# Two moves in the mixing layers of a transformer kernel: the second half of a prepared norm, and the loads of the spatial gate

## The reference, cut to what matters

```
hx = modulated_norm(x, norm_g[l, 1], mx[3], mx[4])     # rmsnorm(x, g) * (1 + scale) + shift
hc = modulated_norm(ctx, norm_g[l, 1], mc[3], mc[4])
px = hx @ w_in[l]                                      # 1024 -> a, b, q, k, v, d and four gates
pc = hc @ w_in[l]                                      # the last layer takes only k and v of ctx
...
# sgu_branch: the spatial gate, b
u, v = split(gelu(p[..., B_OFF:Q_OFF]));  v = layernorm_plain(v)
s = einsum("gpq,bnqgc->bnpgc", w_s, vc) + b_s.T[:, :, None]
yb = (u * s) @ w_b_out
...
merged = g0 * ya + g1 * yb + g2 * yc + g3 * yd         # yc: differential attention over q, k, v
x = x + mx[5] * (merged @ w_o)
```

## Time and profile before

| | us |
|---|---|
| median of 3 runs | 4151.28 |
| the three runs | 4151.28, 4140.68, 4152.42 |
| the profiled execution | 4140.58 |
| its span | 4138.8 |
| TensorE busy | 3803.3 (92%) |
| weight loads busy | 3601.8 (87%) |
| GpSimd busy | 2664.1 (64%) |
| ScalarE busy | 1944.5 (47%) |
| VectorE busy | 1731.4 (42%) |

### The profile page before, as it was taken

The page is one execution under the profiler, slowest core; times in us unless marked ns, Lnnn a source line. Parts: engine busy times, 40 slices in busy tenths (PEclk is TensorE's granted clock), DMA queues, the critical chain, the costliest instruction groups (busy, mean ns, idle before and its releaser), DMA issues.

```text
span 4138.8 us, 93911 instructions
## 1 busy us (share of the span) xinstructions
PE 3803.3 (92%) x36101; PEld 3601.8 (87%) x36101; DVE 1731.4 (42%) x3388; ACT 1944.5 (47%) x2757; POOL 2664.1 (64%) x1186
## 2 busy tenths in 40 slices
PE   8998998997898889899999978879999999997899
PEld 7678987997698757899999868869999999996898
DVE  5543216316633643442222573673223222348442
ACT  5225447433444411545554454464555555545543
POOL 5007873875287300788887747638888888883776
PEclk9999999998899989999999989989999999998999
DMA  5555662663166345566666435426666666652564
GB/s 180 190 195 149 191 179 64 193 166 102 49 192 187 108 165 174 157 187 201 191 191 181 144 88 169 136 75 181 190 192 182 193 184 195 186 168 76 154 176 143
DMA packets 1162942, 664.79 MB, mean 161 GB/s; under 512 B 30157, under 2 KB 1122201, under 8 KB 1162551
## 3 DMA queue, kind: packets, MB, share of 16 engines
q1 hardware_dynamic: 1162679, 661.06, 54.3%
HBM read 659.92 MB, written 1.05 MB: 160 GB/s over the span
## 4 chain that ended last, share of the span: by engine, by line
PE 54%; issue 30%; POOL 11%; DVE 2%; ACT 2%; DMA 1%; POOLq 0%; SPq 0%; DVEq 0%; ACTq 0%
PE bank L855 52%; POOL wlo L615 11%; PE bank L834 1%; PE bank L1056 0%; ACT whi L625 0%; DMA raw<-in_w_in 0%; DVE OUTH L931 0%; PE bank L955 0%; ACT L1932 0%; DMA raw<-in_ffn_w_gu 0%; DVE sq L771 0%; DVE OUTL L933 0%; ACT bank L749 0%; ACT L1940 0%; ACT W L1932 0%
## 5 line engine op out<-in xcount | busy, mean ns | idle before, releaser
L615 POOL TENSOR_TENSOR wlo<-raw,whi 128x1024 fp32r<-128x1024 f32 (+3 forms) x1182 | 2663.9, 2270 | 1450.8 <-ACT whi L625 1444.1
L625 ACT ACTIVATE whi<-raw 128x1024 fp32r<-128x1024 f32 (+3 forms) x1182 | 1172.1, 995 | 1192.0 <-PE bank L855 1002.2
L855 PE MATMUL bank<-AH,whi 128*128 128x256 f32 (+1 forms) x5712 | 1608.5, 282 | 30.3 <-DVE AL L765 10.1
L855 PE MATMUL bank<-AL,whi 128*128 128x256 f32 x5712 | 1600.8, 280 | 0.0
L855 PE MATMUL bank<-AH,wlo 128*128 128x256 f32 (+1 forms) x5712 | 1599.2, 280 | 0.0
L855 PEld LDWEIGHTS bank<-AH,whi 128*128 128x128 f32 x5712 | 1094.8, 192 | 39.4 <-issue 16.5
L855 PEld LDWEIGHTS bank<-AL,whi 128*128 128x128 f32 x5712 | 1090.6, 191 | 0.7
L855 PEld LDWEIGHTS bank<-AH,wlo 128*128 128x128 f32 x5712 | 1089.9, 191 | 0.0
L855 PE MATMUL bank<-HH,whi 128*128 128x256 f32 x1936 | 537.9, 278 | 0.0
L855 PE MATMUL bank<-HL,whi 128*128 128x256 f32 x1936 | 535.9, 277 | 0.0
L855 PE MATMUL bank<-HH,wlo 128*128 128x256 f32 x1936 | 535.9, 277 | 0.0
(11 more groups left out here) (427 smaller groups left out, 5073.5 us busy)
## 6 DMA issues: line engine op xcount, KB each, us to landing
raw<-in_ffn_w SPq DMA_DIRECT2D x420, 512.0 KB, 3.9
raw<-in_w_in SPq DMA_DIRECT2D x182, 512.0 KB, 3.8
raw<-in_ffn_w_gu SPq DMA_DIRECT2D x176, 512.0 KB, 3.8
ada_raw<-in_w_ada SPq DMA_DIRECT2D x96, 512.0 KB, 5.9
raw<-in_ffn_w_down SPq DMA_DIRECT2D x64, 512.0 KB, 3.9
raw<-in_rw_w_rkv SPq DMA_DIRECT2D x48, 512.0 KB, 3.8
raw<-in_w_ada SPq DMA_DIRECT2D x48, 512.0 KB, 5.7
raw<-in_ffn_w SPq DMA_DIRECT2D x56, 384.0 KB, 3.4
```

The lines of the kernel that those rows point to most:

```text
L615: pool.tensor_tensor(wlo[slot][:, 0:n], raw[slot][:, 0:n], whi[slot][:, 0:n], ALU.subtract).then_inc(lo_ready, 1)
L625: act.activation(whi[slot][:, 0:n], raw[slot][:, 0:n], ACT.Copy).then_inc(hi_ready, 1)
L855: mm = pe.matmul(ps[:, 0:o.shape[2]], w, o[:, k0 + c, :], start=tile not in started and c == n == 0, stop=last_panel and c == nk - 1 and n ...
```

## The change

It has two parts. First, for the two hosts mix0c and mix0x the second piece of the prepared norm (the sums over partitions, the root, the reciprocal) stands behind the second tile of `.q` and no longer behind the fourth tile of `.k`. The squares stay behind the first tile of `.k`. TensorE and VectorE get the calls to do so in `.q`. mix1c, which has no `.q`, keeps its place. Second, in all three full mixing layers the spatial gate's loads are issued ahead of the panels of `.ab` and no longer ahead of those of `.q`.

```diff
         for host, name in (("mix0c", "mix0x"), ("mix0x", "f20c")):
-            SUMS_AT[f"{host}.k", 0] = ROOT_AT[f"{host}.k", 3] = name
+            SUMS_AT[f"{host}.k", 0] = ROOT_AT[f"{host}.q", 1] = name
...
-            pe_panels(pe, f"{pre}.q", fills=0)
+            pe_tiles_with_norm(pe, f"{pre}.q", pe_panels(pe, f"{pre}.q", fills=0, by_hand=True))
             pe_panels(pe, f"{pre}.v", fills=0)
...
             if full:
-                dve_tiles(dve, f"{pre}.q", take_copy(dve, DQ))
+                tile = dve_tiles(dve, f"{pre}.q", take_copy(dve, DQ), by_hand=True)
+                for st in range(G[f"{pre}.q"].steps):
+                    tile(st)
+                    dve_prepare(dve, f"{pre}.q", st)
+                dve.wait_ge(bank_free, tiles_of(f"{pre}.q"))
...
-                if g.name.endswith(".q") and g.name[:5] in [f"mix{l}{s}" for l, s in FULL]:
+                if g.name.endswith(".ab") and g.name[:5] in [f"mix{l}{s}" for l, s in FULL]:
                     sp_gated_unit(sp, int(g.name[3]))
```

## The result

The changed kernel takes 4127.98 us in the median of 10 runs (4109.39 to 4151.77), the kernel before 4151.85 in the median of 10. Nine of these ten lie between 4134.17 and 4160.82 us; the tenth took 5591.26, and why isn't known. The ratio of the runs without it is 0.9947, 95% interval 0.9922 to 0.9972: 22 us less, with 12 to 32 us inside the interval.

A forecast was written before the change was run, and what follows sets the result against it. TensorE, busy 3803.3 of 4138.8 us, was taken as the bound; 8.62 + 7.87 + 3.76 - 0.45 - 0.45 gave 19.3 us off, 4121.3 from the profiled execution, 4132 from the median; forecast 4130, range 4116 to 4142.

The forecast's parts named there:

- The cause and the two places in mix0c and mix0x: In mix0c and mix0x, gate loads ahead of the query's first panel make the squares late; removal saves 8.62 and 7.87 us.
- mix1x: In this layer, TensorE's 1.88 us wait ahead of the query and the lower clock behind it go: 3.76 us less.
- Part one gains nothing and costs a little: Sums, root and reciprocal behind the second query tile save nothing and add 0.45 us of wait each in mix0c and mix0x.
- The gate loads ahead of `.ab` cost nothing: At `.ab`'s first panel in three layers, the later issue was priced at nothing, with 3.6 us of cover on ScalarE.
- Rival A: `.ab`'s first panel comes late and TensorE waits in all three layers; gives back 11.3 us, time 4141; chance 8%.
- B: GpSimd's low parts become the bound in the query; gives back 6.6 us, time 4137; chance 8%.
- C: At `.ab`'s first tile, gate transfers hold up the panels behind them; net 6.6 us slower, time 4156; chance 3%.
- D: The query's first panel is late for another reason and the squares stay late; time 4150; chance 3%.
- The sum: Over the three full mixing layers, 8.62 + 7.87 + 3.76 - 0.45 - 0.45 = 19.35, say 19.3 us gained.
- The two levels of the runs: Of three runs of the kernel before, two lay near 4152 us and one near 4141, taken as distinct groups.

The follow-up runs named there:

- loads only: Kernel before with only the gate's loads moved ahead of `.ab`, sums, root and reciprocal left in place: median 4117.75 us, ratio 0.9942.
- root only: Kernel before with only sums, root and reciprocal moved behind the second query tile, gate's loads left ahead of `.q`: median 4137.00 us, ratio 0.9991.
- squares first: Kernel before, but in mix0c and mix0x ScalarE makes the squares ahead of rounding the query's first panel: median 4133.57 us, ratio 0.9973.
- wait left: Kernel before with SyncE's wait for `sgu_free` left ahead of `.q`, only the five gate loads moved ahead of `.ab`: median 4126.84 us, ratio 0.9960.
- six more loads: Changed kernel with six spare loads (640 KB) added behind the gate's five, ahead of `.ab`: one run, 4130.11 us, beside 4136.92 for the kernel before.
- second execution of the changed kernel: The changed kernel profiled again with nothing altered, on the chip of other experiments: median of 12 runs 4120.84 us, ratio 0.9953 to the kernel before.

## Why the prediction was right, point by point

- **The cause and the two places in mix0c and mix0x.** Right, and shown by loads only (all of it), root only (none), and squares first (the link through ScalarE). By the stages, mix0c gave 7.99 us where 8.62 - 0.45 = 8.17 were forecast, mix0x 7.26 where 7.42 were.
- **mix1x.** Forecast 3.76, measured 2.92. In three later profiles with the loads moved the stage takes 30.37 or 30.38 us, which is 34.56 - 30.37 = 4.19 less; in wait left it takes the 31.64 of the first again. The wait is gone in all. What differs is the pace of the tiles, which I had taken as one number, 2.72 us. That 3.76 lies between the two is chance.
- **Part one gains nothing and costs a little.** Right. The wait at the second query tile is 0.26 us instead of 0.45, and the clock stayed at 1.00. The place costs more than its wait, as the tile behind it ran at the slower pace. Counted at 2.72 us a tile, the stages of loads only would be 32.9 to 33.0 us, an estimate from its trace; with both parts they are 33.5. So the term is near 0.5 us a place. It is too small to be told by the timing.
- **The gate loads ahead of `.ab` cost nothing.** Right for the first tile of `.ab`, but not by the cover that was reckoned. The prediction left ScalarE 3.6 us of cover. In the changed kernel's mix0c it had none: it stood for the last panel of the value and then for the first of `.ab`, which landed last:

```profile
2273.86 1.06 ACT L625 ACTIVATE whi<-raw 128x1024 fp32r<-128x1024 f32 x1 [2.65 <-DMA raw<-in_w_in]
2276.91 1.06 ACT L625 ACTIVATE whi<-raw 128x1024 fp32r<-128x1024 f32 x1 [1.99 <-DMA raw<-in_w_in]
```

  The sum took the low part of the buffer's last panel as made right behind its rounding. But GpSimd makes seven low parts in a row behind the squares, and this one is the fourth of them:

```profile
2260.90 16.55 POOL L615 TENSOR_TENSOR wlo<-raw,whi 128x1024 fp32r<-128x1024 f32 x7 [5.01 <-ACT whi L625]
```

  So the buffer came free near 2260.90 + 4 x 2.36 = 2270.3, some 3.7 us later than reckoned, SyncE issued it behind the gate loads at 2271.78, and it landed 5.13 us behind its issue instead of 3.8. What kept TensorE from waiting is the room between low part and use, 3.1 us. That landing was nearer the 5.59 of the earlier trace rows than the median of 3.8. The Trainium skill ("DMA: Bandwidth & Descriptors", "Queues, rings and completion order") ties the completion of a transfer to the earlier writes of the same DMA engine. The 5.13 us agree with that but don't show it: the last panel of the value, issued at 2268.03, just ahead of the gate loads, landed 5.83 us behind its issue, and with six more loads the first of `.ab` took 3.97. Rival A is ruled out for this kernel, with little room beyond.
- **Rivals B, C and D.** B: 0.26 us, far from the 1.88 at which mix1x had lost its clock. C: no wait for a panel at `.ab`; the 0.73 us in mix0x are for VectorE. D: loads only rules it out.
- **The sum.** 19.3 us forecast, 18.2 in the stages of the first profile, 22 (12 to 32) by the timing. The steps that make the gain hold; the largest error of size is the pace in mix1x, 0.84 us, and the wrong cover ahead of `.ab` had no price here.
- **The two levels of the runs.** This remark was wrong. The 35 runs of the kernel before beside the experiments spread from 4124.09 to 4155.07 us without a gap. The three runs that I had were too few to speak of levels. The forecast of 4130 lies near the 4127.98 all the same, since the median of three happened to be near that of ten. That closeness is luck: the spread of single runs is larger than the gain.

## What to carry to other kernels

Look at what an in-order queue holds ahead of the transfer that an engine waits for: a wait for a flag and a few small loads, which TensorE needs only 97 us later (2246.05 to 2342.9 in mix0c), held up a panel, the panel a rounding, the rounding the squares, and the squares TensorE. Small loads belong where their flag has long been up and ahead of a group whose panels have slack. Reckon that slack along the whole row of engines: here ScalarE had none, and only the room behind GpSimd was left. When a wait is named after the last link (here the squares), giving that link more room is worth nothing until the first one is mended. A stretch of the same program without the suspect, here mix1c, prices the stall better than the idle time alone, as it takes in the lower clock behind it.

## What the runs showed of the hardware

At a granted clock of 1.00, the same 24 matmuls take 2.72 us in some stretches and 2.83 in others, 4% more, and which of the two it is differs between executions of the same program. In the 24 stages of the table the pace changed only behind a wait or behind the sums, never within an unbroken row of tiles. VectorE's copies out of two neighbouring tiles of the query in mix1x, in the first and then in the second execution of the changed kernel:

```profile
3628.81 0.42 DVE L903 COPY W<-bank 128x256 f32<-128x256 f32 x1 [2.33 <-PE bank L855]
3631.64 0.42 DVE L903 COPY W<-bank 128x256 f32<-128x256 f32 x1 [2.40 <-PE bank L855]
```

```profile
3629.31 0.42 DVE L903 COPY W<-bank 128x256 f32<-128x256 f32 x1 [2.29 <-PE bank L855]
3632.03 0.42 DVE L903 COPY W<-bank 128x256 f32<-128x256 f32 x1 [2.30 <-PE bank L855]
```

That is 2.83 and 2.72 us a tile. In the kernel before, mix1x went from the slower to the faster pace at its stall, so that removing the stall also removed the switch. Such stretches may be a source of the spread between runs; it was not tested, and what sets the pace stays open.

A stall of 1.88 us in mix1x was followed by a stretch at the lower clock, as were those of 2.00 (squares first) and 2.43 us (root only) in the same place and those of 5.5 us in mix0c and mix0x. Behind waits of 1.03, 1.13, 1.15, 1.49 and 1.72 us (the last two with six more loads) the clock stayed at 1.00, and so it did for the 3 us behind the 1.74 of root only, ahead of its next wait.

VectorE's product of two 128x1024 operands in the rotation took 1.23 us beside an idle GpSimd and 3.31 us beside a busy one, in the rows shown under more loads.
